# Memory units inside the token-major chunks, and the first addition of each FFN group moved

## The reference, cut to what matters

```python
mk = rms_norm(mem, g_mem) @ wk_x             # 256 memory tokens, keys and values
mv = rms_norm(mem, g_mem) @ wv_x
z, xbc, dt_raw, q, k, v = split(rms_norm(x, g_pre_mix) @ w_in)
...                                          # conv and SSD scan on xbc, dt; attention on rope(q), rope(k), v
h = x + rms_norm(concat(y_ssd, y_att) @ w_out, g_post_mix)
...                                          # cross-attention of h into mk, mv
f = (silu(hn @ w_gate) * (hn @ w_up)) @ w_down
h = h + rms_norm(f, g_post_ffn)
```

## Time and profile before

| what | value |
|---|---|
| time, median of 3 runs | 2154.51 us (2154.46 to 2159.66) |
| time of the profiled execution | 2149.75 us, its span 2148.0 us |
| busy: PE, DVE, ACT, POOL | 1984.6, 816.3, 514.4, 509.5 us |
| TensorE's granted clock, mean | 0.949 of full speed |

### The profile page before, as it was taken

The page is one execution under the profiler, slowest core; times in us unless marked ns, Lnnn a source line. Parts: engine busy times, 40 slices in busy tenths (PEclk is TensorE's granted clock), DMA queues, the critical chain, the costliest instruction groups (busy, mean ns, idle before and its releaser), DMA issues.

```text
span 2148.0 us, 29727 instructions
## 1 busy us (share of the span) xinstructions
PE 1984.6 (92%) x12267; PEld 1855.4 (86%) x12267; DVE 816.3 (38%) x1618; ACT 514.4 (24%) x1248; POOL 509.5 (24%) x300
## 2 busy tenths in 40 slices
PE   7999999877688779899899989999999999999997
PEld 7999899766567679899788989999999999999995
DVE  5345015585676641520432163132122212312327
ACT  5100112275466441421331142100100000010002
POOL 4442442131000012122001213313213222231323
PEclk9999999897678889999998999999999999999998
DMA  5331331101400431111434121111101101110122
GB/s 209 115 119 66 102 134 40 61 25 46 141 1 1 165 119 46 74 65 50 170 145 155 52 79 61 48 40 49 50 20 59 39 29 49 39 49 29 59 95 110
DMA packets 55975, 161.26 MB, mean 75 GB/s; under 512 B 4160, under 2 KB 17984, under 8 KB 54464
## 3 DMA queue, kind: packets, MB, share of 16 engines
q1 hardware_dynamic: 33280, 115.04, 14.8%
q10 hardware_dynamic: 22592, 44.81, 6.0%
HBM read 131.67 MB, written 28.16 MB: 74 GB/s over the span
## 4 chain that ended last, share of the span: by engine, by line
PE 78%; DVE 10%; ACT 5%; issue 3%; DMA 2%; POOL 1%; SPq 0%; ACTq 0%; DVEq 0%; POOLq 0%
PE bank L226 22%; PE bank L229 22%; PE bank L230 22%; DVE at_sm L1632 2%; PE bank L929 2%; PE bank L940 1%; PE bank L899 1%; PE bank L264 1%; DVE ACC L1866 1%; DMA H<-scratch_h 1%; DVE H L327 1%; POOL w_lo L516 1%; PE bank L709 1%; DVE MT L1573 1%; DVE E L1566 1%
## 5 line engine op out<-in xcount | busy, mean ns | idle before, releaser
L514 POOL CAST w_hi<-w_raw 128x1024 fp32r<-128x1024 f32 x130 | 140.8, 1083 | 1500.3 <-PE bank L226 1353.2
L226 PE MATMUL bank<-OH,w_hi 128*128 128x384 f32 x1056 | 357.8, 339 | 0.0
L229 PE MATMUL bank<-OL,w_hi 128*128 128x384 f32 x1056 | 357.6, 339 | 0.0
L230 PE MATMUL bank<-OH,w_lo 128*128 128x384 f32 x1056 | 357.5, 339 | 0.0
L516 POOL TENSOR_TENSOR w_lo<-w_raw,w_hi 128x1024 fp32r<-128x1024 f32 x130 | 323.3, 2487 | 10.4
L230 PE MATMUL bank<-w_hi,NL 128*128 128x256 f32 x864 | 244.9, 283 | 0.0
L1849 DVE TENSOR_TENSOR hr<-sg,bank 128x384 f32<-128x384 f32 x66 | 36.6, 554 | 448.6 <-PE bank L230 447.6
L226 PEld LDWEIGHTS bank<-OH,w_hi 128*128 128x128 f32 x1056 | 198.1, 188 | 0.4
L229 PEld LDWEIGHTS bank<-OL,w_hi 128*128 128x128 f32 x1056 | 198.1, 188 | 0.4
L230 PEld LDWEIGHTS bank<-OH,w_lo 128*128 128x128 f32 x1056 | 198.1, 188 | 0.0
L226 PE MATMUL bank<-w_hi,NH 128*128 128x256 f32 x576 | 163.5, 284 | 6.8 <-POOL w_lo L516 6.8
(11 more groups left out here) (327 smaller groups left out, 3853.9 us busy)
## 6 DMA issues: line engine op xcount, KB each, us to landing
w_raw<-in_wall SPq DMA_DIRECT2D x130, 512.0 KB, 3.2
scratch_h<-H ACTq DMA_DIRECT2D x6, 1536.0 KB, 5.3
cK<-in_cmk SPq DMA_DIRECT2D x8, 1024.0 KB, 6.8
cV<-in_cmv SPq DMA_DIRECT2D x8, 1024.0 KB, 4.8
H<-in_x SPq DMA_DIRECT2D x1, 4608.0 KB, 14.5
H<-scratch_h SPq DMA_DIRECT2D x1, 4608.0 KB, 17.7
Hback<-scratch_h ACTq DMA_DIRECT2D x1, 4608.0 KB, 14.0
out_y<-Hback SPq DMA_DIRECT2D x9, 512.0 KB, 2.6
```

The costliest lines, as they stand in the source:

```text
L226: m = mm(out, ah, bh, start=(i == 0), stop=False)
L229: mm(out, ah, bl, start=False, stop=False)
L230: m = mm(out, al, bh, start=False, stop=(i == n - 1))
L514: pool.tensor_copy(whi[s][:], raw[s % 2][:]).then_inc(w_hi, 1)
```

## The change

The memory units move from behind the chunks into them. `hosted` says which chunk holds which units and `mem_at` ahead of which token unit each stands; the items of `wall` and their slots are reordered to match. A memory unit in chunk j uses the pair of slots that the chunk's own two items don't use; the token unit behind it counts the release (`freed`). ACT's copies are reordered alike. POOL's first memset (`one`), from which the counts of `w_hi` started, goes away. In the FFN, DVE's first addition of each group moves ahead of that group's last `hid_l`.

```diff
-        one = sb("one", [P, 1])
...
+        tm_items = (0, 2, 4, 10, 14, 18, 22, 26)
+        mk_items = (6, 7, 8, 9, 12, 13, 16, 17)
+        mv_items = (20, 24, 28, 30)
+        hosted = {2: (0, 1, 2, 3), 3: (4, 5), 4: (6, 7), 5: (8, 9), 6: (10, 11), 7: (12, 13, 14, 15)}
+        mem_at = {2: (2, 3, 4, 5), 3: (4, 6), 4: (4, 6), 5: (4, 6), 6: (4, 6), 7: (3, 4, 8, 8)}
...
+        def freed(units):
+            return bool(units) and (units[-1] < KT or units[-1] % 2 == 1)
...
-                s = n % 4
-
+                s = n % 4 if n < 8 or n >= I_XB else (2, 3, 2, 3, 0, 1, 0, 1)[n % 8]
...
                 for t in range(NT):
+                    for n in mem_units(j, t):
+                        mem_unit(n, (j + 1) % 2)
...
-                          release=((0,) if t == 0 and kind + jj else (4,) if t == NT - 1 else ())).then_inc(tm_mm, 1)
+                          release=(((0,) if (t == 0 and kind + jj) or freed(mem_units(j, t)) else ()) +
+                                   ((4,) if t == NT - 1 else ()))).then_inc(tm_mm, 1)
...
+            def mem_unit(n, pair):
+
+                if n == 0:
+                    pe.wait_ge(p_lo, 2 * Z_J1)
+                if n == 10:
+                    pe.wait_ge(s_dt, 1)
+                if n >= 2:
                     pe.wait_ge(mem_ev, n - 1)
...
+                if n < KT:
+                    s = 2 * pair + n % 2
+                    pe.wait_ge(w_ready, I_TM + mk_items[n] + 1)
...
+                else:
+                    j, t, s = (n - KT) // 2, n % 2, 2 * pair
+                    pe.wait_ge(w_ready, I_TM + mv_items[j] + 2)
...
+                    release = (4,) if t else ()
+                three(B[6 + n % 2][:, 0:256], pairs, release=release).then_inc(mem_mm, 1)
...
-                for i in range(4):
-                    if kind < 2:
-                        mem_k(4 * kind + i)
-                    elif i % 2:
-                        mem_v(2 * (kind - 2) + i // 2)
...
-                    pe.wait_ge(mem_ev, 12)
+                    pe.wait_ge(mem_ev, 10)
...
                 for t in range(start, NT):
+                    for n in mem_units(j, t):
+                        mem_out_unit(n)
                     tm_evac(kind, jj, t, f)
                 store(kind, jj)
...
             act.dma_start(g("wdr")[:], wdt).then_inc(ld["one"], 16)
-            for m in range(4):
-                mem_k_out(m)
             act.wait_ge(setup, 2)
...
             act.wait_ge(ld["one"], 32)
             act_f(g("wdh")[:], g("wdr")[:], ACT.Copy).then_inc(s_dtu, 1)
+            for n in hosted[2]:
+                mem_out_unit(n)
             store(1, 0)
+            for n in hosted[3]:
+                mem_out_unit(n)
             store(1, 1)
...
-            hidden(0)
-            for gi in range(1, NG):
-                hidden(gi)
-                for q in range(2 * NT):
-                    add_down(gi - 1, q, B[6 + q % 2])
+            for gi in range(NG):
+                for n in range(6 * gi, 6 * gi + 5):
+                    hid_raw(n)
+                    hid_low(n)
+                hid_raw(6 * gi + 5)
+                if gi:
+                    add_down(gi - 1, 0, B[6])
+                hid_low(6 * gi + 5)
+                if gi:
+                    for q in range(1, 2 * NT):
+                        add_down(gi - 1, q, B[6 + q % 2])
...
-    wall = np.concatenate([mix[0:4], wk[0:4], mix[4:8], wk[4:8], mix[8:12], wv[0:4], mix[12:16], wv[4:8],
+    wall = np.concatenate([mix[0:6], wk[0:4], mix[6:8], wk[4:6], mix[8:10], wk[6:8], mix[10:12], wv[0:2], mix[12:14],
+                           wv[2:4], mix[14:16], wv[4:8],
```

More of the change, by code:

```diff
@@ L396, in tm_no, with mem_units @@
             return 18 * kind + 9 * jj + t
+        tm_items = (0, 2, 4, 10, 14, 18, 22, 26)
[3 more added lines that the diff above has]
+        mem_at = {2: (2, 3, 4, 5), 3: (4, 6), 4: (4, 6), 5: (4, 6), 6: (4, 6), 7: (3, 4, 8, 8)}
+        def mem_units(j, t):
+            return [n for n, at in zip(hosted.get(j, ()), mem_at.get(j, ())) if at == t]
+        def freed(units):
+            return bool(units) and (units[-1] < KT or units[-1] % 2 == 1)
         s_dt, s_dtm, s_dtc, s_dtu = sem("dt_ready"), sem("dt_mm"), sem("dt_copies"), sem("dt_act")
@@ L503, in _ @@
         def _(pool):
-            pool.memset(one[:], 1.0).then_inc(w_hi, 1)
-            pool.wait_ge(w_hi, 1)
             def split(n):
-                s = n % 4
+                s = n % 4 if n < 8 or n >= I_XB else (2, 3, 2, 3, 0, 1, 0, 1)[n % 8]
                 pool.wait_ge(w_raw[s % 2], 16 * (n // 2 + 1))
@@ L514, in split @@
                 pool.tensor_copy(whi[s][:], raw[s % 2][:]).then_inc(w_hi, 1)
-                pool.wait_ge(w_hi, n + 2)
+                pool.wait_ge(w_hi, n + 1)
                 pool.tensor_tensor(wlo[s][:], raw[s % 2][:], whi[s][:].bitcast(F32), ALU.subtract).then_inc(w_ready, 1)
@@ L557, in tm_chunk @@
                 s = 2 * jj
-                pe.wait_ge(w_ready, I_TM + 8 * kind + 2 * jj + 2)
+                j = 2 * kind + jj
+                pe.wait_ge(w_ready, I_TM + tm_items[j] + 2)
                 for t in range(NT):
+                    for n in mem_units(j, t):
+                        mem_unit(n, (j + 1) % 2)
                     if kind + jj == 0:
@@ L568, in tm_chunk @@
                             wlo[s + k // 4][:, 256 * (k % 4):256 * (k % 4) + 256]) for k in range(KT)],
-                          release=((0,) if t == 0 and kind + jj else (4,) if t == NT - 1 else ())).then_inc(tm_mm, 1)
+                          release=(((0,) if (t == 0 and kind + jj) or freed(mem_units(j, t)) else ()) +
+                                   ((4,) if t == NT - 1 else ()))).then_inc(tm_mm, 1)
                     if kind + jj == 0 and t + 2 < NT:
                         pre_trans(pe, Z_X + t + 2, g("H")[:, t + 2, :])
[L573 to L586, removed]
-                    pe.wait_ge(mem_ev, n - 1)
[L588 to L592, removed]
+            def mem_unit(n, pair):
[4 more added lines that the diff above has]
+                if n >= 2:
+                    pe.wait_ge(mem_ev, n - 1)
+                if n < KT:
+                    s = 2 * pair + n % 2
+                    pe.wait_ge(w_ready, I_TM + mk_items[n] + 1)
+                    pairs = [(whi[s][:, tok(k)], wlo[s][:, tok(k)], g("mhi")[:, k, :], g("mlo")[:, k, :])
+                             for k in range(KT)]
+                    release = ()
+                else:
+                    j, t, s = (n - KT) // 2, n % 2, 2 * pair
+                    pe.wait_ge(w_ready, I_TM + mv_items[j] + 2)
+                    pairs = [(g("mhi")[:, k, tok(t)], g("mlo")[:, k, tok(t)],
+                              whi[s + k // 4][:, 256 * (k % 4):256 * (k % 4) + 256],
+                              wlo[s + k // 4][:, 256 * (k % 4):256 * (k % 4) + 256]) for k in range(KT)]
+                    release = (4,) if t else ()
+                three(B[6 + n % 2][:, 0:256], pairs, release=release).then_inc(mem_mm, 1)
@@ L1040, in tm_out, with mem_out_unit @@
                 for t in range(start, NT):
+                    for n in mem_units(j, t):
+                        mem_out_unit(n)
                     tm_evac(kind, jj, t, f)
                 store(kind, jj)
[L1044 to L1052, removed]
+            def mem_out_unit(n):
+                j, t = (n - KT) // 2, n % 2
+                dst = g("mraw")[:, n, :] if n < KT else g("mvs")[:, t, 256 * j:256 * j + 256]
+                act.wait_ge(mem_mm, n + 1)
+                act_f(dst, B[6 + n % 2][:, 0:256], ACT.Copy).then_inc(mem_ev, 1)
             for t in range(NT):
@@ L1082, in _ @@
             act_f(g("wdh")[:], g("wdr")[:], ACT.Copy).then_inc(s_dtu, 1)
+            for n in hosted[2]:
+                mem_out_unit(n)
             store(1, 0)
+            for n in hosted[3]:
+                mem_out_unit(n)
             store(1, 1)
-            for m in range(4, KT):
-                mem_k_out(m)
+            for n in hosted[4]:
+                mem_out_unit(n)
             act.wait_ge(mem_ev, KT)
@@ L1089, in _ @@
             store(2, 0)
+            for n in hosted[5]:
+                mem_out_unit(n)
             store(2, 1)
-            for j in range(2):
-                mem_v_out(j)
             for c in range(CH):
@@ L1105, in _ @@
             tm_out(3, 1, ACT.Silu)
-            for j in range(2, 4):
-                mem_v_out(j)
             act.wait_ge(mem_ev, 2 * KT)
@@ L1840, in _, with hid_raw, hid_low @@
             ACC = g("ACC")
[L1842 to L1852, removed]
+            def hid_raw(n):
+                dve.wait_ge(f_sg, n + 1)
+                dve.wait_ge(f_up, 2 * n + 2)
+                if n >= 2:
+                    dve.wait_ge(f_hh, n - 1)
+                TT(g(f"hr{n % 2}")[:], g(f"sg{n % 2}")[:], B[2 * (n % 3) + 1][:, 0:NC], ALU.mult).then_inc(f_hr, 1)
+            def hid_low(n):
+                gi, c, f = n // 6, n % 6 // 2, n % 2
+                dve.wait_ge(f_hh, n + 1)
```

(2 more changed lines are left out.)

## The result

The changed kernel took **2125.74 us** (median of 4 runs, 2123.53 to 2127.13) against 2155.2 us before: a ratio of 0.9858, with a 95% interval of 0.9841 to 0.9875. It is 1.4% faster, where 2145.1 us (0.44%) was predicted, in a range of 2139 to 2151. The direction was right and the size was off by 19 us. The profiled execution took 2123.53 us.

A forecast was written before the change was run, and what follows sets the result against it. PE, busy 92% of the span, was taken as the bound; 10.49 us of removed stops less 1.09 us for a new one gave 9.4 us, so 2154.51 - 9.4 = 2145.1 us, range 2139 to 2151.

The forecast's parts named there:

- What goes away: Projection: PE's two long stops, two short waits for POOL and the wait ahead of `dt` vanish, 10.49 us in all.
- no new stops: Projection chunks and entry to the `xbc` loop: POOL's splits finish before PE needs them, with slacks such as 2.7 us.
- the new stop: Entry of the `xbc` loop: PE now waits for ACT's copy of the unit just ahead, costing 1.09 us.
- the second stop: Projection, PE idle from 154.44 to 158.82 us; with the lower clock behind it, 5.89 us to be gained.
- The sum: Projection: 10.49 us gained less 1.09 us for the loop's entry, 9.4 us out.
- The memset saved at the start lies ahead of the first load: Kernel start: POOL's dropped memset of `one` precedes the first load; no time was counted for it.
- A start to start distance is 0.12 us: Projection: spacing of matmul starts at 256 columns, 24 to a unit; 2.82 us was used for every unit.
- zero, both ways: FFN: moving the first addition earlier frees nobody and the delayed `hid_l` holds nobody up, so no gain or loss.
- The rotary work: Rival, projection chunks 2 to 5: DVE's rotary additions slow beside POOL's splits, 3 us back, 2148.2 us; chance 0.05.
- POOL's splits: Rival, projection: late splits delay all behind them; 5.33 us each costs 2.5 us, from 8.0 us slower overall; chance 0.04.
- Given back later: Rival, stages behind the projection: lower clock and short stops take 3 to 4 us, about 2149 us; chance 0.11.
- Covers: Projection: ACT's waits for the `wdr` and `cvi` loads, the latter about 5 us, are hidden by PE's queued work.

The follow-up runs named there:

- e2_order: Changed kernel with the FFN order of before and an unused 32-byte tile where `one` stood, leaving only the memory units' new places: 2145.97 us, ratio 0.9948.
- e2_pad64: Changed kernel with the FFN order of before and an unused 64-byte tile where `one` stood: 2138.94 us, ratio 0.9921 to the kernel before.
- e2_all64: Changed kernel with the FFN order of before and an unused 64-byte tile ahead of the weights' tiles, which move along: 2114.01 us, ratio 0.9794.
- e5_hid0: Changed kernel with the FFN order of before, only the FFN's `hid` tiles moved to offset 0 modulo 256 to the weights: 2108.42 us, ratio 0.9788.
- e1_ffn_old: Changed kernel with the FFN order of the kernel before on DVE: 2114.55 us, ratio 0.9822 to the kernel before.
- e4_release: Changed kernel, FFN order kept, first weight slot released in a group's second down product instead of the first: 2116.85 us, ratio 0.9821.

## Why the prediction was wrong

- **What goes away, no new stops, the new stop: right.** With the addresses and the FFN order of before, none of the four waits for POOL and no wait ahead of `dt` is left, and the granted clock from 60 to 300 us is 1.00. (Behind the second stop of the kernel before the distance did not double: it rose from 0.1175 to 3.40 / 16 = 0.2125 us, and the sum used that.) The loop's entry cost 291.44 - 290.41 - 0.12 = 0.91 us and 0.10 for the second matmul, 1.01 against 1.09. The sum was 9.4; the loop came 9.41 us earlier and the median fell by 10.7. That the two agree to the hundredth is luck: 0.30 us of the 9.41 lie ahead of the projection's first matmul (18.44 us in the kernel before, 18.14 here).
- **"The memset saved at the start lies ahead of the first load": the step that failed.** The prediction priced the memset, not the tile. It saw in the diff that `one` goes and did not ask what is allocated behind it. That term was put at nothing; the runs showed 31.4 us for it, three times the sum.
- **"A start to start distance is 0.12 us", 2.82 us for every unit in both kernels:** the form in which the same mistake entered the sum. In chunk 7 a unit took 24 x 0.1133 = 2.72 us afterwards. No row of the kernel before alone could show it; the addresses could have been laid beside each other.
- **FFN "zero, both ways": wrong, 11.2 us.** It asked who waits for the first addition and who for the delayed `hid_l`, but not what is queued behind `hid_l` on DVE: the second addition, one product ahead of PE. And it had the row for the cost in hand: the contention of the earlier trace rows was weighed against the rotary work and not against the other DVE instruction that the change moves beside POOL.
- **Rivals.** The rotary work did not fall behind: of the two additions, 36 each from 60 to 300 us, the first took a mean of 614 ns (549 before) and the second 439 (438 before), and PE waited for no rotary copy:

```profile
L1497 DVE TENSOR_TENSOR stg<-rpA,rpB 128x128 f32<-128x128 f32 x36 | 22.1, 614 | 1.2
L1498 DVE TENSOR_TENSOR stg<-rpA,rpB 128x128 f32<-128x128 f32 x36 | 15.8, 439 | 0.0
```

  POOL's splits were in time. Given back later: not by the medians. In the one profiled execution of e2_order some 6 of the 9.4 us were lost again behind 300 us (its span is 2144.6 us, 3.4 less than before's; matmul by matmul the lead is 3.3 us from 1290 us on); that pair is one execution each, and the profiled one of before lay 5 us under its median.
- **Covers.** ACT waited 2.8 us for `wdr` and 11.0 us for `cvi` (5 predicted); PE waited for neither.

## What to carry to other kernels

A diff that adds, removes or resizes a tile moves every tile allocated behind it. Where PE is the bound and its stream has thousands of matmuls, compare the distance of matmul starts by shape before and after, and try a few pads between the weights' tiles and the rest: here an unused 32 bytes was worth three times the whole rescheduling. And when an instruction of one engine is moved, name both what queues behind it and what runs beside it at the new place.

## What the runs showed of the hardware

- **The distance of matmuls depends on where their two operands lie to each other.** At a granted clock of 1.00 (the 2.4 GHz level) in the FFN, 384 columns take 0.173 to 0.177 us and 512 columns 0.227 to 0.234; in the projection 256 columns take 0.1133 to 0.120 us, by an offset of less than 256 bytes. e2_pad64 against e2_all64 shows that it is the offset, and e5_hid0, at 512 columns, that it is that of the matmul's own operands. The Trainium skill, "SBUF — State Buffer", section "Who interferes with whom", gives TensorE two independent read ports, for the moving operand and for the weight load, and says that TensorE waits for nobody. Two independent ports give no reason for the up to 7 ns a matmul that were measured between offsets. What exactly costs them, the reading or something else, no run shows. The same page's section "Operand start alignment" speaks of legality alone.
- **At one offset there are two distances at 256 columns, kept over whole units.** At offset 64 they are 0.1133 and 0.1178 us (each the mean of 23 distances). In the changed kernel all units that start from 48 to 89 us have 0.1178 (two right behind transposes aside); in e1_ffn_old, with the same instructions and addresses up to there, those from 48.9 to 83 us have 0.1133 (the same two aside). They change at unit boundaries. The kernel before, at offset 96, has 0.1173 and 0.1187 in its token units. e2_all64, e5_hid0 and e4_release spent more units at 0.1178 than e1_ffn_old. What chooses is open. It may be part of the 7 to 12 us by which runs at offset 64 differ among themselves, but the kernel before spreads by 10 us too (2150.3 to 2160.2 beside e1_ffn_old).
